# Memory attention of a two-block transformer kernel: where the squares of the state are summed, and the order of the heads' turns and values

## The chip, the cores and the metric

The kernel runs on one core of one Trainium2 chip. The metric is the device time of one execution in microseconds; three runs of the kernel before gave a median of 2088.11 us (2086.93 to 2088.28). The whole computation is one launch with one instruction stream per engine: TensorE (PE), VectorE (DVE), ScalarE (ACT), GpSimd (POOL), and SyncE (SP), which only issues the transfers.

## The reference, cut to what matters

The kernel computes two blocks (a convolution and forgetting attention, a cross attention to a memory, an MLP, and then a second block) on 512 tokens of width 1024. The change lies in the cross attention of the first block:

```python
def memory_cross_attention(h, mem_n, w_mq, w_mk, w_mv, w_mo):      # h = rms_norm(x, norm_mem_pre)
    q = (h @ w_mq).reshape(B, S, MEM_HEADS, MEM_HEAD_DIM)          # 512 tokens, 4 heads of 128
    k = (mem_n @ w_mk).reshape(B, N_MEM, MEM_HEADS, MEM_HEAD_DIM)  # 256 memory rows
    v = (mem_n @ w_mv).reshape(B, N_MEM, MEM_HEADS, MEM_HEAD_DIM)
    logits = jnp.einsum("bqhd,bmhd->bhqm", q, k) * (MEM_HEAD_DIM ** -0.5)
    p = jax.nn.softmax(logits, axis=-1)
    out = jnp.einsum("bhqm,bmhd->bqhd", p, v).reshape(B, S, MEM_INNER)
    return out @ w_mo

def rms_norm(x, g):
    return x * rsqrt(mean(x * x, -1) + 1e-6) * g
```

The root of the mean square of a token is a factor on all its logits. The kernel therefore forms `q` from `x * g` alone, and multiplies the logits by the token's factor inside the exponential.

## The kernel before, in words

State and activations lie feature by feature: eight tiles of 128 features by 512 tokens. Every fp32 product is made of three products of parts (high times low, low times high, high times high, `mm3`), so one 128x128 by 512 step of a product is three matmuls. After each product that feeds another, ACT copies the PSUM bank to a rounded high part and DVE subtracts it to get the low part (`high` and `low`).

Each engine has its own instruction list, written out by hand, and runs it in order. Semaphores that are counted through names (`up`, `at`) connect the lists. PSUM has eight banks, which TensorE takes in turn; `open_bank` waits until the tenant of eight banks ago is free. There is no planner: what stands next in an engine's list runs next, or blocks those behind it.

The stage at issue, on TensorE (lines 981 to 1010):

- `mem_v`: values of the memory. `mem_q(n)`: the queries of head n, eight steps or 24 matmuls; heads 0 and 1 are made together first. `mem_s(h)`: the logits of head h, four blocks of 128 tokens by 256 memory rows, 12 matmuls into two banks. It needs the high part of the queries (ACT, `mq_high`) and the low part (DVE, `mq_out`).
- `column_sum` of the tiles in its list: for each tile four products of 128 tokens with a matrix of ones of 96 columns, so that token sums land one per partition. The four products of a tile are fp32, and each shows as two matmul records. Here it sums the one tile `Y1[0]`, into which DVE has added the squares of all eight tiles of the state (`add_squares`, the last of its seven additions is named `hacc 1 7`).
- `mem_t(h)`: eight transposes that turn the probabilities (tokens by memory rows) of head h. It needs the normalised probabilities, of which ACT makes block 0 (`mem_norm`) and DVE blocks 1 to 3 (`mem_rcp`). `mem_pv(h)`: the values weighted with them, six matmuls, which needs both parts of the turned probabilities (`mem_turned` on ACT, `mem_low` on DVE).
- then `gemm("wm")`, the output product with `w_mo`, 96 matmuls in two chunks of weights of 48.

On ACT (lines 1738 to 1761): `root` takes the square root of the sums, `mem_exp(h)` four exponentials with their sums, and the functions named above. The exponential of head h waits for the head's negated and scaled maximum. On DVE (lines 2515 to 2545): `inverse` (reciprocal of the root), two multiplications that make the scales, `mem_max` (two maxima for a head), `mem_scale` (maxima times scale), and the functions named above. `mem_out(h)` on ACT and DVE makes the two parts of a head's output from the bank of `mem_pv(h)`, and frees it.

POOL makes the low parts of most weights at this place: `w_mq`'s second chunk, then `w_mo`'s first, each in four pieces.

Of the kernel before, what the change touches and what calls it, by code (L numbers as in the profile page):

```python
# [286 lines left out]
def build(nc, t):  # L287
# [9 lines left out]
    with es:  # L297
# [214 lines left out]
        def tensor_program(pe):  # L512
# [35 lines left out]
            def column_sum(parts, nb=4, first=0):  # L548


                for group, ap, need, freed, done in parts:
                    ps = bank(*group) if group in begun else open_bank(*group, hold=True)
                    pe.wait_ge(*at(*need))
                    for b in range(nb):
                        ins = pe.mm(ps[:, SUMW * b:SUMW * b + SUMW], ap[:, blk(first + b)], ONE[:, 0:SUMW],
                                    group not in begun and b == 0,
                                    done is not None, shared=True)
                    begun.add(group)
                    if freed and done:
                        ins.then_inc(*up(acc, ("tf", *freed), done))  # L560
                    elif freed:
                        ins.then_inc(*up(acc, ("tf", *freed)))
                    elif done:
                        ins.then_inc(*up(acc, done))
                    if done:
                        close(*group)
# [377 lines left out]
            def mem_q(n):  # L944
                w = CH["w_mq"][1]
                wh, wl = chunk(w)
                ps = open_bank("mq", n)
                for k in range(8):
                    col = (2 * k + n % 2) * 128
                    pe.wait_ge(*at("hn", 1, k))  # L950
                    ins = pe.mm3(ps[:], wh[:, col:col + 128], wl[:, col:col + 128], *feat(k), k == 0, k == 7)
                ins.then_inc(*up(acc, ("mq", n), *[("w_used", w)] * (n % 2)))

            def mem_s(h):
                for i in range(4):
                    c = 256 * (i % 2)
                    if c == 0:
                        ps = open_bank("ms_", h, i // 2)
                    pe.wait_ge(*at("qm", h))
                    pe.wait_ge(*at("km", h))  # L960
                    ins = pe.mm3(ps[:, c:c + 256], QMH[:, h, blk(i)], QML[:, h, blk(i)], KMH[:, h, :], KML[:, h, :],
                                 True, True)
                    if c:
                        ins.then_inc(*up(acc, ("ms_", h, i // 2)))

            def mem_t(h):
                for j in range(2):
                    ps = open_bank("mt", h, j)
                    for i in range(4):
                        pe.wait_ge(*at("mp", h, i))  # L970
                        ins = pe.turn(ps[:, blk(i)], PM[h % 2][:, i, blk(j)], IDT[:])
                    ins.then_inc(*up(acc, ("mt", h, j)))

            def mem_pv(h):
                ps = open_bank("mo", h)
                for j in range(2):
                    pe.wait_ge(*at("pm", h, j))
                    pe.wait_ge(*at("vm", j))
                    ins = pe.mm3(ps[:], VMH[:, j, blk(h)], VML[:, j, blk(h)], PMH[h % 2][:, j, :], PML[h % 2][:, j, :],
                                 j == 0, j == 1)  # L980
                ins.then_inc(*up(acc, ("mo", h)))
# [10 lines left out]
                close("mq", n)  # L992
            mem_v(1, 1)
            mem_s(0)
            mem_q(2)
            mem_s(1)
            column_sum([(("st", 1), Y1[:, 0, :], ("hacc", 1, 7), None, ("st", 1))])
            mem_q(3)
            mem_s(2)
            mem_t(0)  # L1000
            mem_t(1)
            mem_s(3)
            mem_pv(0)
            mem_t(2)
            mem_pv(1)
            mem_t(3)
            mem_pv(2)
            mem_pv(3)
# [332 lines left out]
        def scalar_program(act):  # L1341
# [364 lines left out]
            def mq_high(n):  # L1706
                act.wait_ge(*at("mq", n))
                high(QMH[:, n, :], bank("mq", n)[:], ("qm", n))

            def mem_exp(h):  # L1710
                slot = 32 * (h % 2) + 160
                for i in range(4):
                    if h >= 2:
                        act.wait_ge(*at("mt", h - 2, 1))
                    act.wait_ge(*at("max", "ms_", h))
                    act.act(PM[h % 2][:, i, :], bank("ms_", h, i // 2)[:, 256 * (i % 2):256 * (i % 2) + 256], ACT.Exp,
                            SM[:, 20 + i:21 + i], SM[:, slot + i:slot + i + 1], SM[:, slot + 4 + i:slot + 5 + i]).then_inc(
                        *out(("exp", "ms_", h, i), *[("free", "ms_", h, i // 2)] * (i % 2)))

            def mem_norm(h):  # L1720

                for i in range(1):
                    s, p = 32 * (h % 2) + 168 + i, PM[h % 2][:, i, :]
                    act.wait_ge(*at("rcp", "ms_", h))
                    act.act(p, p, ACT.Identity, SM[:, s:s + 1]).then_inc(*out(("mp", h, i)))

            def mem_turned(h):
                for j in range(2):
                    act.wait_ge(*at("mt", h, j))
                    if h >= 2:  # L1730
                        act.wait_ge(*at("mo", h - 2))
                    high(PMH[h % 2][:, j, :], bank("mt", h, j)[:], ("pm", h, j))

            def mem_out(h):
                act.wait_ge(*at("mo", h))
                high(OMH[:, h, :], bank("mo", h)[:], ("om", h))
# [3 lines left out]
            mem_v_high(0)  # L1740
            mem_v_high(1)
            weights(CH["w_mo"][0])
            mq_high(2)
            root(("st", 1), 0, "eps6")
            mem_exp(0)
            mem_norm(0)
            mem_exp(1)
            mq_high(3)
            mem_norm(1)
            mem_turned(0)  # L1750
            mem_exp(2)
            mem_turned(1)
            mem_norm(2)
            mem_exp(3)
            mem_out(0)
            mem_turned(2)
            mem_norm(3)
            mem_out(1)
            mem_turned(3)
            mem_out(2)  # L1760
            mem_out(3)
# [321 lines left out]
        def vector_program(dve):  # L2083
# [375 lines left out]
            def add_squares(s, Y, start=1, end=7):  # L2459

                for k in range(start, end + 1):
                    dve.wait_ge(*at("hsq", s, k))
                    if k > 1:
                        dve.wait_ge(*now(dve_tile))
                    dve.tt(Y[:, 0, :], Y[:, 0, :], Y[:, k, :], ALU.add).then_inc(*out(("hacc", s, k)))
# [7 lines left out]
            def mem_v_low(b):  # L2473
                low(VML[:, b, :], bank("mv", b)[:], VMH[:, b, :], ("vm", b), ("free", "mv", b))

            add_squares(1, Y1, 1, 2)


            def mq_out(n):
                low(QML[:, n, :], bank("mq", n)[:], QMH[:, n, :], ("qm", n), ("free", "mq", n))  # L2480

            def mem_max(h):

                s = 32 * (h % 2) + 160
                for b in range(2):
                    dve.wait_ge(*at("ms_", h, b))
                    dve.rmax(SM[:, s + 2 * b:s + 2 * b + 2],
                             bank("ms_", h, b)[:].rearrange("p (a c) -> p a c", a=2)).then_inc(*out(("mmax", h)))

            def mem_scale(h):  # L2490

                s = 32 * (h % 2) + 160
                dve.wait_ge(*at("mmax", h))
                dve.wait_ge(*at("mscale"))
                dve.tt(SM[:, s:s + 4], SM[:, s:s + 4], SM[:, 24:28], ALU.mult).then_inc(*out(("max", "ms_", h)))
# [11 lines left out]
            def mem_low(h):  # L2507
                for j in range(2):
                    low(PML[h % 2][:, j, :], bank("mt", h, j)[:], PMH[h % 2][:, j, :], ("pm", h, j),
                        ("free", "mt", h, j))  # L2510

            def mem_out(h):
                low(OML[:, h, :], bank("mo", h)[:], OMH[:, h, :], ("om", h), ("free", "mo", h))
# [2 lines left out]
            mq_out(1)  # L2516
            mem_v_low(0)
            mem_v_low(1)
            add_squares(1, Y1, 3, 7)
            mem_max(0)  # L2520
            mq_out(2)
            mem_max(1)
            inverse(("st", 1), 0, [("rs1",)])
            dve.wait_ge(*at("rs1"))
            dve.ts(SM[:, 24:28], SM[:, 4:8], -MEM_SCALE, None, ALU.mult).then_inc(*out())
            dve.ts(SM[:, 20:24], SM[:, 4:8], MEM_SCALE, None, ALU.mult).then_inc(*out(("mscale",)))
            mem_scale(0)
            mem_scale(1)
            mem_rcp(0)
            mem_rcp(1)  # L2530
            mq_out(3)
            mem_max(2)
            mem_scale(2)
            mem_low(0)
            mem_max(3)
            mem_scale(3)
            mem_rcp(2)
            mem_low(1)
            mem_rcp(3)
            mem_out(0)  # L2540
            mem_low(2)
            mem_out(1)
            mem_low(3)
            mem_out(2)
            mem_out(3)
# [1067 lines left out]
```

## Time and profile before

| what | value |
|---|---|
| three runs, median (lowest to highest) | 2088.11 us (2086.93 to 2088.28) |
| the profiled execution, its time | 2087.23 us |
| the profiled execution, its span | 2085.4 us |
| TensorE clock granted in it, mean | 0.992 |
| PE busy, share of the span | 2009.2 us, 96% |
| DVE busy | 1271.7 us, 61% |
| ACT busy | 858.6 us, 41% |
| POOL busy | 983.8 us, 47% |

PE, PEld, DVE, ACT, POOL and SP are TensorE's matmuls, its weight loads, VectorE, ScalarE, GpSimd and SyncE. L159 is line 159 of the kernel, often that of a helper: L158 and L159 are where all matmuls are issued, L167 the transposes, L182 all two-tensor operations, L173, L175 and L176 ACT's operations. Tiles are named without their numbers, so `Y` holds the squares, `QMH` and `QML` the two parts of the queries, `KMH` and `KML` those of the keys, `PM` the probabilities, `PMH` and `PML` the two parts of the turned ones, `OMH` and `OML` those of the output, `SM` the small vectors. Matmuls are pipelined: a record is longer than the step from its start to the next start. Times in a timeline are from the start of the span.

### The profile page before, as it was taken

The numbers are of one execution on the slowest core, as the hardware profiler recorded it, in microseconds if no ns is written. First come the engines' busy times: TensorE is split into PE (matmuls) and PEld (weight loads), VectorE is DVE, ScalarE is ACT, GpSimd is POOL, SyncE is SP. The second block draws the span as 40 slices with busy tenths as digits, with TensorE's granted clock in tenths as the row PEclk, the third lists the DMA queues.
The fourth block names the chain that finished last, engine by engine and source line by source line (L and its number), as shares of the span: only waits on it lengthen the run. The fifth ranks groups of instructions, "written<-read, shape, count | busy, mean of one in ns | idle before, by whom it ended". The sixth has DMA issues, their size and how long they took to land.

```text
span 2085.4 us, 23731 instructions
## 1 busy us (share of the span) xinstructions
PE 2009.2 (96%) x9691; PEld 1672.7 (80%) x9691; DVE 1271.7 (61%) x1568; ACT 858.6 (41%) x1250; POOL 983.8 (47%) x486
## 2 busy tenths in 40 slices
PE   7999999899999999999999999999998999999997
PEld 5777888788888877887888888878887888888886
DVE  8678727452344445562777775455579667777643
ACT  5847764621122235773433333242322244333322
POOL 5578554453444333113444444345667644444443
PEclk9999999999999999999999999999999999999999
DMA  6422123112222221021122222224222312223221
GB/s 206 176 104 81 62 82 115 67 61 101 101 88 95 101 98 44 22 71 61 61 101 101 96 88 100 101 81 171 82 71 101 122 66 96 101 101 101 82 101 41
DMA packets 35040, 193.00 MB, mean 93 GB/s; under 512 B 4399, under 2 KB 4991, under 8 KB 15412
## 3 DMA queue, kind: packets, MB, share of 16 engines
q1 hardware_dynamic: 34932, 191.49, 26.2%
q8 instruction: 76, 1.25, 0.3%
q14 instruction: 32, 0.26, 0.0%
HBM read 177.77 MB, written 13.64 MB: 92 GB/s over the span
## 4 chain that ended last, share of the span: by engine, by line
PE 81%; DVE 10%; ACT 4%; POOL 3%; issue 1%; DMA 0%; ACTq 0%; SPq 0%; DVEq 0%; POOLq 0%
PE ps L159 77%; PE ps L158 4%; DVE TMP L182 1%; POOL WL L182 1%; DVE X L182 1%; DVE ps L194 1%; DVE X L194 1%; PE ps L167 1%; DVE YL L182 1%; POOL YF L182 1%; ACT WH L175 0%; DVE VG L182 0%; ACT PM L173 0%; DVE HL L194 0%; POOL CO L182 0%
## 5 line engine op out<-in xcount | busy, mean ns | idle before, releaser
L182 POOL TENSOR_TENSOR WL<-W,WH 128x2048 fp32r<-128x2048 f32 (+3 forms) x172 | 648.3, 3776 | 867.2 <-ACT WH L175 863.7
L159 PE MATMUL ps<-HH,WL 128*128 128x512 f32 (+1 forms) x1392 | 539.1, 387 | 17.1 <-DVE HL L194 7.9
L159 PE MATMUL ps<-HL,WH 128*128 128x512 f32 (+1 forms) x1392 | 532.4, 382 | 0.0
L159 PE MATMUL ps<-HH,WH 128*128 128x512 f32 (+1 forms) x1392 | 532.4, 382 | 0.0
L175 ACT ACTIVATE WH<-W 128x2048 fp32r<-128x2048 f32 (+2 forms) x144 | 267.6, 1858 | 312.9 <-PE ps L159 312.9
L159 PEld LDWEIGHTS ps<-HH,WL 128*128 128x128 f32 x1392 | 262.2, 188 | 76.1 <-DVE HL L194 9.9
L159 PEld LDWEIGHTS ps<-HH,WH 128*128 128x128 f32 x1392 | 262.1, 188 | 51.6
L159 PEld LDWEIGHTS ps<-HL,WH 128*128 128x128 f32 x1392 | 262.3, 188 | 49.5 <-issue 0.2
L182 DVE TENSOR_TENSOR MRL<-MID,MRH 128x512 fp32r<-128x512 f32 x76 | 177.4, 2366 | 162.3 <-ACT MRH L175 162.3
L159 PE MATMUL ps<-MRH,WL 128*128 128x512 f32 x608 | 238.1, 392 | 3.3 <-ACT PAD L175 2.2
L159 PE MATMUL ps<-MRH,WH 128*128 128x512 f32 x608 | 236.7, 389 | 0.0
L159 PE MATMUL ps<-MRL,WH 128*128 128x512 f32 x608 | 236.6, 389 | 0.0
L182 DVE TENSOR_TENSOR MID<-TMP,TMP 128x512 f32<-128x512 f32 x44 | 175.9, 3997 | 30.7 <-ACT TMP L176 30.7
L175 ACT ACTIVATE PAD<-ps 128x512 f32<-128x512 f32 x88 | 52.6, 601 | 273.0 <-PE ps L159 273.0
L194 DVE SCALAR_TENSOR_TENSOR TMP<-PAD,PAR,TMP 128x512 f32<-128x512 f32 x176 | 140.8, 800 | 6.2
L159 PEld LDWEIGHTS ps<-MRH,WL 128*128 128x128 f32 x608 | 114.2, 188 | 28.5 <-ACT PAD L175 3.0
L159 PEld LDWEIGHTS ps<-MRH,WH 128*128 128x128 f32 x608 | 114.1, 188 | 24.0
L159 PEld LDWEIGHTS ps<-MRL,WH 128*128 128x128 f32 x608 | 114.2, 188 | 23.6 <-issue 0.5
L194 DVE SCALAR_TENSOR_TENSOR X<-X,ps 128x512 f32<-128x512 f32 (+1 forms) x36 | 22.5, 628 | 110.3 <-PE ps L159 110.2
L182 POOL TENSOR_TENSOR TMP<-TMP,TMP 128x512 f32<-128x512 f32 x47 | 62.4, 1327 | 57.3 <-ACT TMP L176 55.5
L182 DVE TENSOR_TENSOR TMP<-ps,TMP 128x512 f32<-128x512 f32 x36 | 24.8, 689 | 104.8 <-PE ps L159 98.3
L188 DVE TENSOR_SCALAR TMP<-PAD,PAR 128x512 f32<-128x512 f32 x88 | 42.3, 481 | 72.2 <-ACT PAD L175 72.2
(368 smaller groups left out, 3317.1 us busy)
## 6 DMA issues: line engine op xcount, KB each, us to landing
W<-in_up SPq DMA_DIRECT2D x44, 1024.0 KB, 4.8
W<-in_down SPq DMA_DIRECT2D x22, 1024.0 KB, 4.8
W<-in_w_up SPq DMA_DIRECT2D x16, 1024.0 KB, 4.8
W<-in_w_down SPq DMA_DIRECT2D x16, 1024.0 KB, 4.8
W<-in_hy_in SPq DMA_DIRECT2D x12, 1024.0 KB, 4.9
kd<-STG SPq DMA_DIRECT2D x36, 256.0 KB, 2.0
KB<-kd SPq DMA_DIRECT2D x8, 1024.0 KB, 5.3
W<-in_win_ag SPq DMA_DIRECT2D x4, 1024.0 KB, 5.2
```

Source lines behind the costliest of these rows:

```text
L158: return self.eng.matmul(out, lhs, rhs, start=start, stop=stop, skip_group_check=True)
L159: return self.eng.matmul(out, lhs, rhs, start=start, stop=stop)
L167: return QUIET if self.eng is None else self.eng.transpose(out, src, ident)
L175: return self.eng.activation(out, src, fn, scale=scale)
L182: return QUIET if self.eng is None else self.eng.tensor_tensor(out, a, b, op)
L188: return self.eng.tensor_scalar(out, a, s1, None, o1)
L194: return self.eng.scalar_tensor_tensor(out=out, in0=a, scalar=s, in1=b, op0=o1, op1=o2)
```

## The change

Three things change, in this one stage.

1. DVE adds only the squares of tiles 1 to 3 into `Y1[0]`, all three ahead of `mq_out(0)` (before: two there, and five behind `mem_v_low(1)`). TensorE sums `Y1[0]` and the tiles 4 to 7 by themselves in one group of five column sums, placed right behind `mem_s(0)` (before: one column sum behind `mem_s(1)`).
2. The order of turns and values on TensorE: `mem_t(0)` ahead of `mem_q(3)`, `mem_t(1)` ahead of `mem_s(2)`, `mem_pv(0)` ahead of `mem_s(3)`, `mem_pv(1)` ahead of `mem_t(2)`.
3. The lists of ACT and DVE follow: the root, the exponentials and the normalisation of head 0 stand ahead of the queries of head 2, those of head 1 ahead of the queries of head 3; `mem_out(0)` on DVE stands ahead of `mem_rcp(3)`.

```diff
@@ tensor_program
             mem_v(1, 1)
             mem_s(0)
+            column_sum([(("st", 1), Y1[:, 0, :], ("hacc", 1, 3), None, None),
+                        *[(("st", 1), Y1[:, k, :], ("hsq", 1, k), None, ("st", 1) if k == 7 else None)
+                          for k in range(4, 8)]])
             mem_q(2)
             mem_s(1)
-            column_sum([(("st", 1), Y1[:, 0, :], ("hacc", 1, 7), None, ("st", 1))])
+            mem_t(0)
             mem_q(3)
+            mem_t(1)
             mem_s(2)
-            mem_t(0)
-            mem_t(1)
+            mem_pv(0)
             mem_s(3)
-            mem_pv(0)
+            mem_pv(1)
             mem_t(2)
-            mem_pv(1)
             mem_t(3)
             mem_pv(2)
             mem_pv(3)
@@ scalar_program
             weights(CH["w_mo"][0])
-            mq_high(2)
             root(("st", 1), 0, "eps6")
             mem_exp(0)
             mem_norm(0)
+            mq_high(2)
             mem_exp(1)
-            mq_high(3)
             mem_norm(1)
             mem_turned(0)
+            mq_high(3)
+            mem_turned(1)
             mem_exp(2)
-            mem_turned(1)
             mem_norm(2)
             mem_exp(3)
             mem_out(0)
-            mem_turned(2)
             mem_norm(3)
             mem_out(1)
+            mem_turned(2)
             mem_turned(3)
@@ vector_program
-            add_squares(1, Y1, 1, 2)
+            add_squares(1, Y1, 1, 3)
@@
             mem_v_low(1)
-            add_squares(1, Y1, 3, 7)
             mem_max(0)
-            mq_out(2)
-            mem_max(1)
             inverse(("st", 1), 0, [("rs1",)])
             dve.wait_ge(*at("rs1"))
             dve.ts(SM[:, 24:28], SM[:, 4:8], -MEM_SCALE, None, ALU.mult).then_inc(*out())
             dve.ts(SM[:, 20:24], SM[:, 4:8], MEM_SCALE, None, ALU.mult).then_inc(*out(("mscale",)))
             mem_scale(0)
+            mem_rcp(0)
+            mq_out(2)
+            mem_max(1)
             mem_scale(1)
-            mem_rcp(0)
             mem_rcp(1)
+            mem_low(0)
             mq_out(3)
+            mem_low(1)
             mem_max(2)
             mem_scale(2)
-            mem_low(0)
             mem_max(3)
             mem_scale(3)
             mem_rcp(2)
-            mem_low(1)
+            mem_out(0)
             mem_rcp(3)
-            mem_out(0)
+            mem_out(1)
             mem_low(2)
-            mem_out(1)
             mem_low(3)
```

## Rows read from the trace of the kernel before

**Rows 1.** The page: busy time, and the chain that ended last, by engine.
```profile
PE 2009.2 (96%) x9691; PEld 1672.7 (80%) x9691; DVE 1271.7 (61%) x1568; ACT 858.6 (41%) x1250; POOL 983.8 (47%) x486
PE 81%; DVE 10%; ACT 4%; POOL 3%; issue 1%; DMA 0%; ACTq 0%; SPq 0%; DVEq 0%; POOLq 0%
```
**Rows 2.** Busy time by stretch: the stage from mem_s(0) to the output product.
```profile
351.68:383.83 32.15, 27.77 (x162) 23.42 (x160) 25.33 (x52) 21.76 (x54) 6.65 (x5) 1.00 0.20 66
```
**Rows 3.** What PE waited for, 350 to 388: total, times, longest.
```profile
PE ps L167 <- ACT PM L176: 3.2, 3, 1.5
PE ps L159 <- ACT PM L173: 0.9, 1, 0.9
```
**Rows 4.** Timeline of PE: start us, us, operation [idle before <-releaser].
```profile
351.68 0.28 PE L159 MATMUL ps<-KMH,QML 128*128 128x256 f32 x1
...
353.11 0.40 PE L159 MATMUL ps<-HH,WL 128*128 128x512 f32 x1
...
358.58 0.28 PE L159 MATMUL ps<-KMH,QML 128*128 128x256 f32 x1
...
360.49 1.10 PE L158 MATMUL ps<-ONE,Y 128*128 128x96 f32 x8 [0.32 <-DVE Y L182]
361.38 0.48 PE L159 MATMUL ps<-HH,WL 128*128 128x512 f32 x1
361.70 0.39 PE L159 MATMUL ps<-HL,WH 128*128 128x512 f32 x1
...
366.94 0.28 PE L159 MATMUL ps<-KMH,QML 128*128 128x256 f32 x1
...
368.37 1.03 PE L167 MATMUL ps<-IDT,PM 128*128 128x128 f32 x8
...
380.07 1.09 PE L167 MATMUL ps<-IDT,PM 128*128 128x128 f32 x8 [1.49 <-ACT PM L176]
380.93 0.48 PE L159 MATMUL ps<-PMH,VML 128*128 128x512 f32 x1
...
383.83 0.39 PE L159 MATMUL ps<-OMH,WL 128*128 128x512 f32 x1
```
**Rows 5.** Timeline of PE, a column sum of three tiles.
```profile
405.59 2.81 PE L158 MATMUL ps<-ONE,TMP 128*128 128x96 f32 x24
```
**Rows 6.** Timeline of DVE.
```profile
347.09 3.47 DVE L182 TENSOR_TENSOR Y<-Y 128x512 f32<-128x512 f32 x2
350.48 1.27 DVE L182 TENSOR_TENSOR QML<-ps,QMH 128x512 fp32r<-128x512 f32 x2
...
370.81 1.28 DVE L207 TENSOR_REDUCE SM<-ps 128x2 f32<-128x512 f32 x2
```
**Rows 7.** Shortest, median and longest of the squares' additions, 346 to 362.
```profile
L182 DVE TENSOR_TENSOR Y<-Y x5: 692/1659/1772, 347.1 to 355.3; 128x512 f32<-128x512 f32 x5
```
**Rows 8.** Timeline of POOL.
```profile
344.87 6.84 POOL L182 TENSOR_TENSOR WL<-W,WH 128x512 fp32r<-128x512 f32 x4
...
388.03 4.60 POOL L182 TENSOR_TENSOR WL<-W,WH 128x2048 fp32r<-128x2048 f32 x1 [26.56 <-ACT WH L175]
```
**Rows 9.** Timeline of ACT.
```profile
361.63 0.26 ACT L176 ACTIVATE SM<-ps,PAR 128x4 f32<-128x4 f32 x1 [2.25 <-PE ps L158]
361.92 1.28 ACT L173 ACT_TABLE_LOAD   x1
363.93 0.56 ACT L173 ACTIVATE PM<-ps,SM 128x256 f32<-128x256 f32 x1 [0.73 <-DVE SM L182]
364.49 0.56 ACT L173 ACTIVATE PM<-ps,SM 128x256 f32<-128x256 f32 x1
...
372.31 0.57 ACT L173 ACTIVATE PM<-ps,SM 128x256 f32<-128x256 f32 x1 [1.29 <-DVE SM L182]
...
379.45 0.57 ACT L176 ACTIVATE PM<-PM,SM 128x256 f32<-128x256 f32 x1
379.85 0.66 ACT L175 ACTIVATE OMH<-ps 128x512 fp32r<-128x512 f32 x1
```

## The prediction, made before the result was known

> **What bounds the kernel now.** The page comes first: PE is busy for 96% of the span and holds 81% of the chain that ended last [rows 1]. So PE time that is added anywhere is paid for unless PE was waiting there, and a wait is worth at most what PE stands idle. Second, the stretch of the change, from `mem_s(0)` at 351.68 to the first matmul of the output product at 383.83: 32.15 us, PE busy for 27.77, so 4.38 idle, at the full granted clock (1.00, which is 2.4 GHz) [rows 2]. Third, what PE waited for: 3.2 us in three waits before transposes, for the normalised probabilities, and 0.9 before `mem_pv(0)` [rows 3]; before the column sum that the change makes earlier it is only 0.32 [rows 4]. Fourth, the timelines of the engines, to see which wait ends last. Behind the stage PE starts 96 matmuls of the output product, and all that follows depends on them; so the change is worth what it does to the start at 383.83.
>
> **The prices.** From starts [rows 4]: `mem_s` 353.11 - 351.68 = 1.43 us; `mem_q(2)` 358.58 - 353.11 = 5.47; `mem_q(3)`, behind another kind of matmul, 366.94 - 361.38 = 5.56, as its first step takes 0.32 instead of 0.23; eight transposes 380.93 - 380.07 = 0.86. A column sum of one tile takes 361.38 - 360.49 = 0.89. The one of three tiles lasts 2.81 to the end of its last record [rows 5]; from 361.38 against 360.49 + 1.10 a last record reaches 0.21 us past the next start, so that is 2.60, or 0.87 a tile. I take 0.885 for a tile, 4.42 us for five.
>
> **Part 1, the squares.** The change adds four tiles, 32 matmul records, 3.53 us of PE. It takes four additions from DVE, which are on no list that PE waits for except the column sum's own. In return the sum stands earlier. But a third addition now stands ahead of `mq_out(0)`, and behind that low part are `mq_out(1)`, `mem_v_low` and all of DVE's list; on PE `mem_s(0)` waits for it, and everything behind. In the trace two additions last from 347.09 to 350.56, `mq_out(0)` starts at 350.48 and `mem_s(0)` 1.20 later, with no idle time before it [rows 4, 6]. The third addition costs between 0.69 (the shortest of these rows) and 1.77 (the longest) [rows 7]. The long ones run while POOL makes low parts of weights, from 344.87 to 351.71 [rows 8]; the third would start at 350.58, inside that. I take the long one: the addition ends at 352.35, `mq_out(0)` at 352.98 (0.68 after a start at 352.30), `mem_s(0)` starts at 353.02, 1.34 late, and I let its first step cost 0.1 more, as the first behind another kind did at 361.38. By the short end PE would wait 0.3 us instead.
>
> The Trainium skill (SBUF — State Buffer, Who interferes with whom) says that the port pair that VectorE and GpSimd share is an exclusive lock: a VectorE instruction with two SBUF inputs waits for the whole of a GpSimd instruction that reads SBUF. The trace agrees, since additions come at 0.69 or at about 1.66 us and none between [rows 7], and by it the third addition waits until POOL is done at 351.71 and ends at 352.4, as taken. If the two shared bandwidth instead, it would end at about 352.0 and the sum below would be 0.35 less.
>
> **Part 2, PE's list up to the logits of head 2.** From 351.68: wait and restart 1.44, `mem_s(0)` 1.43, five column sums 4.42 (done 358.97), `mem_q(2)` 5.56 (done 364.53), `mem_s(1)` 1.43 (365.96), `mem_t(0)` 0.87 (366.83), `mem_q(3)` 5.56 (372.39), `mem_t(1)` 0.86 (373.25), `mem_s(2)` 1.51, as it follows transposes and its first step costs 0.08 more (374.76). Nothing in this list waits a second time: the probabilities of head 0 are there early, as follows, and those of head 1 at about 371. In the kernel before `mem_s(2)` ended at 368.37 [rows 4]. So it is 6.4 us late.
>
> **Part 3, the scale, sooner.** The root starts at 359.15 instead of 361.63. In the kernel before the table load of 1.28 lay beside DVE's work and the first exponential waited another 0.73 for DVE [rows 9]; now DVE waits with `mem_scale(0)` right behind the inverse, and the table load is what is late: `mem_exp(0)` starts at 360.75, 3.2 us sooner than 363.93. That gain ends there. `mem_exp(1)` needs the logits of head 1, which PE finishes at 365.96 behind the column sums and `mem_q(2)`, and DVE must first make `mq_out(2)`, which waits until ACT's `mq_high(2)` can start at 364.7. DVE: 365.3 to 365.9, two maxima to 367.1, scale; `mem_exp(1)` starts at about 367.3, where it started at 366.89. Head 1 is then normalised at about 370.5, so `mem_t(1)` finds it ready.
>
> **Part 4, from the logits of head 2 to the end.** `mq_high(3)` starts at 372.57, `mq_out(3)` 373.19 to 373.79, two `mem_low(1)` to 374.99, then `mem_max(2)`. From there to the exponential it was 372.31 - 370.81 = 1.50 [rows 6, 9]; so `mem_exp(2)` starts at 376.49, 4.18 us later than before. The rest was 383.83 - 372.31 = 11.52 us [rows 4, 9]. Now, counted from `mem_exp(2)`: four exponentials at about 0.55, then reciprocal and normalisation of 0.40 [rows 9], `mem_exp(3)` at +2.93 (its maxima are ready at +1.9), `mem_out(0)` on ACT at +5.12 and on DVE to +6.35, only then `mem_rcp(3)`, the normalisation at +6.56, `mem_out(1)` at +6.97, `mem_turned(2)` at +7.46; DVE's `mem_out(1)` to +8.19 and its first `mem_low(2)` to +8.87; `mem_pv(2)` and `mem_pv(3)` take 383.83 - 380.93 = 2.90 [rows 4], so the output product starts at +11.81, 0.29 more. Before, `mem_exp(3)` stood 3.54 behind `mem_exp(2)`, but its reciprocal did not wait for `mem_out(0)`: the gain of one is lost by the other. The wait for the transposes of head 3 grows from 1.49 to about 3.0 us.
>
> **The sum.** 4.18 + 0.29 = 4.5 us, the product's start at 388.3. Check by PE alone: 3.53 added, and waits of 4.38 become about 5.4 (1.4 before `mem_s(0)`, about 1 before `mem_t(2)`, 3 before `mem_t(3)` and `mem_pv(2)`). The second chunk of `w_mo` is no new wait: POOL has its low part at 388.03 + 4.60 = 392.63 [rows 8], PE wants it 48 steps of 0.227 after 383.83, at 394.7, and both move together, since ACT's copy stands behind the last `mem_out`. No transfer is moved. Nothing downstream has slack that PE's start could eat, PE being busy for 96%. Against the profiled execution, 2087.23 + 4.5 = 2091.7; the median of the runs shown is 0.9 above that execution, so 2088.11 + 4.5 = **2092.6 us**. Ends: the short third addition takes off 1.0 (3.4); a bank or a queue that I ordered wrongly by one operation of 0.6 on the path from head 2 adds 0.6 to 1.2 (5.7).
>
> **Rivals.**
> (a) *The waits absorb it.* PE stood idle for 4.38 us and 3.53 is added; if the earlier scale moves the whole chain of probabilities by its 3 us, all exponentials start early, PE's waits before the transposes go, and the added work lies in their place: from nothing to +0.9, 2088.1 to 2089.0. For it: the three waits before transposes are the largest [rows 3]. Against: only head 0 is early; heads 1 and 2 wait for PE itself.
> (b) *The other side, not slower.* The same mechanism to its end: PE never waits from 351.68 on and needs only 27.77 + 3.53 = 31.30 us, 0.85 less than now: 2087.3. It decides from the point where `mem_exp(2)` starts by 371. Against: the third addition alone gives PE a new wait, and `mem_s(2)` is behind 23 us of PE's work. Even so it is within 0.2%.
> (c) *Cheap column sums.* A record of 96 columns steps at 0.11 us [rows 4, 5]. If in a long group its 96 columns alone set the pace, 0.04 us each at 2.4 GHz, the 40 records would take 1.6 instead of 4.4, and the sum falls to +1.7: 2089.8. Against: the 24 of one group kept 0.11, and so do records of other widths, the transposes of 128 columns with 0.86/8 = 0.107 and the logits of 256 with 1.43/12 = 0.119 [rows 4]; something that all have in common, not the columns, sets it. The Trainium skill (TensorE: Matmul & The Clock Gate, Back-to-back issue gap) has about 81 ns for a pair of weight load and matmul at 128 columns; by that the 40 records take 3.2 us, an estimate, and the forecast falls to +3.3, 2091.4. No row of this trace shows that pace.
> (d) *More than forecast.* DVE's queue from `mem_low(1)` to `mem_max(2)`, and `mem_out(0)` ahead of `mem_rcp(3)`, each wait for ACT, which waits for PE: if one of these hand-overs is missed, +5.7 to +7, 2093.8 to 2095.
>
> **How the numbers follow.** About 0.2% (4.2 us) is what a measurement of this kernel can tell from no change. The forecast (+3.4 to +5.7) has 0.74, of which I put 0.48 above 4.2 us and 0.26 below, since 4.5 is close to that bound. (a) has 0.10, (b) 0.03, (c) 0.03, (d) 0.08, and 0.02 is left for faster by a cause that I don't see. Slower: 0.48 + 0.08 = 0.56; same: 0.26 + 0.10 + 0.03 + 0.03 = 0.42; faster 0.02. The range adds half a microsecond of the runs' spread to both ends and leaves out (a), (b) and half of (d): 2090.6 to 2094.3.
>
> **What would show it.** An idle time of 1.0 to 1.4 us before `mem_s(0)`, with a low part of the queries as its releaser; a group of 40 records of 128x96 from about 354.5, 4.4 us long; the table load between root and first exponential with no wait behind it; `mem_s(2)` ending 6 us later than 368.37, `mem_exp(2)` at about 376.5; one long wait of about 3 us before the transposes of head 3; the first matmul with `OMH` at 388.3. A start of the product below 386 would make the prediction wrong, and if `mem_exp(2)` is then early, its third and fourth part.

## The result and the profile after

The changed kernel takes 2093.76 us (median of nine runs, 2091.8 to 2095.16) against 2088.11 (nine runs, 2086.36 to 2089.06): 1.0028 times the time, 95% interval 1.002 to 1.0036, so 5.65 us more. The forecast was 2092.6, in the range 2090.6 to 2094.3. The profiled execution took 2091.94 us with a span of 2090.1, the second fastest of the nine. The median lies 1.8 above it, and that turns out to matter.

The page of after, span and busy time, in the columns of [rows 1]:
```profile
span 2090.1 us, 23786 instructions
PE 2010.9 (96%) x9723; PEld 1673.4 (80%) x9723; DVE 1267.7 (61%) x1564; ACT 859.1 (41%) x1250; POOL 982.3 (47%) x486
```
Exactly 32 matmul records more on PE and four instructions fewer on DVE. Spans are not the place to read the difference, though: the stage begins at 353.39 here and at 351.68 before, with no line changed ahead of it that TensorE waits for (e10, whose only edit lies in the stage, begins it at 353.15), and it ends 2090.1 - 390.36 = 1699.7 us before the span does, against 2085.4 - 383.83 = 1701.6. These two differences, +1.7 and -1.9 us, nearly cancel in this pair. So each kernel below is read by the length of its stage, from the end of the last `mem_v` product (its last start plus 0.227) to the first matmul of the output product.

The stage of after, to hold against [rows 2] (columns: PE, PEld, DVE, ACT, POOL busy, granted clock, DMA share, GB/s):
```profile
353.39:390.36 36.97, 32.46 (x194) 28.26 (x194) 21.40 (x49) 22.31 (x54) 4.97 (x5) 0.95 0.17 58
385.00:388.40 3.40, 3.24 (x12) 2.76 (x13) 3.25 (x7) 2.65 (x6) 0.00 (x0) 0.55 0.00 0
```
It lasts 36.97 us instead of 32.15: 4.82 more. And the clock column is new: 0.95 over the stage and 0.55 in its last part, where it was 1.00.

PE's timeline of after, answering to [rows 4]:
```profile
354.62 0.39 PE L159 MATMUL ps<-KMH,QML 128*128 128x256 f32 x1 [1.06 <-DVE QML L182]
...
356.16 2.82 PE L158 MATMUL ps<-ONE,Y 128*128 128x96 f32 x24
358.81 1.95 PE L158 MATMUL ps<-ONE,Y__178 128*128 128x96 f32 x16
360.54 0.47 PE L159 MATMUL ps<-HH,WL 128*128 128x512 f32 x1
...
376.20 0.40 PE L159 MATMUL ps<-PMH,VML 128*128 128x512 f32 x1
...
381.14 1.14 PE L167 MATMUL ps<-IDT,PM 128*128 128x128 f32 x8 [0.57 <-ACT PM L176]
385.16 1.97 PE L167 MATMUL ps<-IDT,PM 128*128 128x128 f32 x8 [2.88 <-ACT PM L176]
386.97 0.79 PE L159 MATMUL ps<-PMH,VML 128*128 128x512 f32 x1
387.56 0.63 PE L159 MATMUL ps<-PML,VMH 128*128 128x512 f32 x1
...
390.36 0.39 PE L159 MATMUL ps<-OMH,WL 128*128 128x512 f32 x1
```
`mem_s(0)` starts 354.62 - 353.39 = 1.23 us late, behind the low part of the queries. The 40 records of column sums take 360.54 - 356.16 = 4.38. `mem_s(2)` ends at 376.20, which is 22.81 of the stage against 16.69 before, 6.12 later. PE does not wait from `mem_s(0)` until the transposes of head 2 (0.57), and waits 2.88 before those of head 3. Those eight transposes take 386.97 - 385.16 = 1.81 instead of 0.86, and the values of heads 2 and 3 390.36 - 386.97 = 3.39 instead of 2.90. The slow transposes cost the stage nothing here: in e6 below they take 0.86, and PE then waits 0.67 for VectorE's low part, so the values of head 2 start no sooner.

ACT's timeline of after, answering to [rows 9]:
```profile
361.08 1.28 ACT L173 ACT_TABLE_LOAD   x1
362.37 0.56 ACT L173 ACTIVATE PM<-ps,SM 128x256 f32<-128x256 f32 x1
...
369.06 0.56 ACT L173 ACTIVATE PM<-ps,SM 128x256 f32<-128x256 f32 x1 [2.15 <-DVE SM L182]
...
378.04 0.56 ACT L173 ACTIVATE PM<-ps,SM 128x256 f32<-128x256 f32 x1 [2.37 <-DVE SM L182]
```
Counted from the start of the stage, the first exponential of head 0 stands at 8.98 (12.25 before, 3.3 sooner), that of head 1 at 15.67 (15.21 before), that of head 2 at 24.65 (20.63 before, 4.02 later). The gain of the earlier scale ends at the first head. The additions of squares, answering to [rows 7]: all three that are left are slow ones, the third too.
```profile
L182 DVE TENSOR_TENSOR Y<-Y x3: 1665/1665/1773, 348.8 to 352.3; 128x512 f32<-128x512 f32 x3
```

### The profile page after: what moved, and what is told of

It reads as the page before. It is cut to its first block, busy times and chain, and to the rows that moved or that the text cites. A ratio compares the mean times of both kernels' runs of the same rounds, so it can differ in the third digit from the quotient of the medians.

```text
span 2090.1 us, 23786 instructions
## 1 busy us (share of the span) xinstructions
PE 2010.9 (96%) x9723; PEld 1673.4 (80%) x9723; DVE 1267.7 (61%) x1564; ACT 859.1 (41%) x1250; POOL 982.3 (47%) x486
## 4 chain that ended last, share of the span: by engine, by line
PE 80%; DVE 10%; POOL 4%; ACT 4%; issue 1%; DMA 0%; ACTq 0%; SPq 0%; DVEq 0%; POOLq 0%
PE ps L159 76%; PE ps L158 4%; DVE TMP L182 1%; POOL WL L182 1%; DVE X L182 1%; DVE ps L194 1%; PE ps L167 1%; POOL X L182 1%; DVE X L194 1%; DVE YL L182 1%; POOL YF L182 1%; DVE HL L194 1%; ACT WH L175 0%; DVE VG L182 0%; POOL CO L182 0%
## 5 line engine op out<-in xcount | busy, mean ns | idle before, releaser
L159 PEld LDWEIGHTS ps<-MRH,WL 128*128 128x128 f32 x608 | 114.1, 188 | 28.4 <-ACT PAD L175 3.0
```

The lines of the kernel that those rows point to most:

```text
L159: return self.eng.matmul(out, lhs, rhs, start=start, stop=stop)
```

## The experiments

Two notions of the loss are tested: PE's own order with its added work (the theory), and either part by itself being the whole of it. From e5 on, the half clock is a question of its own.

**e1, the sums alone.** The five early sums with the turns and values in the order of before (TensorE's part of the edit is shown; the lists of ACT and DVE follow it).
```diff
 mem_s(0); column_sum(five tiles)
-mem_q(2); mem_s(1); mem_t(0); mem_q(3); mem_t(1); mem_s(2); mem_pv(0); mem_s(3); mem_pv(1); mem_t(2); mem_t(3)
+mem_q(2); mem_s(1); mem_q(3); mem_s(2); mem_t(0); mem_t(1); mem_s(3); mem_pv(0); mem_t(2); mem_pv(1); mem_t(3)
```


> The five early column sums alone (three additions on VectorE, tiles 4 to 7 on TensorE, root and inverse ahead of the queries of head 2), turns and values of the heads in the order of before. The stage from mem_s(0) to the output product was 32.15 us before and 36.97 after. Theory (the change costs by TensorE's own order: 3.53 us of added matmuls, 1.3 us of waiting for the third addition, and turns that now stand ahead of the logits of heads 2 and 3): one turn less stands ahead of mem_s(2), so mem_exp(2) starts about 2 us sooner than after; stage 34.3 us, +2.1 over before, time about 2090.5. Rival (the early sums are all of the loss, the order is free): stage about 37, +4.8, time 2093. Rival (the early sum helps by itself and the new order spoils it): stage under 32.

Measured: stage 34.73 us (+2.58), time 2091.33 us, 1.0013 of before (1.0003 to 1.0022). `mem_exp(2)` at 23.21 of the stage, 1.44 sooner than after. The clock is 1.00 throughout the stage (the stage's busy times, then what PE waited for):
```profile
353.30:388.03 34.73, 31.19 (x193) 27.07 (x193) 20.89 (x49) 21.89 (x54) 4.96 (x5) 1.00 0.18 62
```
```profile
PE ps L167 <- ACT PM L176: 2.4, 2, 1.5
```
```profile
374.35 1.91 PE L167 MATMUL ps<-IDT,PM 128*128 128x128 f32 x16
```
Both turns, not one, have left the place ahead of `mem_s(2)`: its end, where these transposes start, is at 374.35 - 353.30 = 21.05 of the stage, 1.76 sooner than after. From `mem_exp(2)` to the output product it is 34.73 - 23.21 = 11.52 us, as before. One limit of the edit: on ACT the exponentials of head 0 still stand behind `mq_high(2)`, so `mem_exp(0)` starts at 368.12, 14.82 of the stage (12.25 before). The early sum brings no early exponential here, and the rival that it would help by itself isn't tested in full. An estimate bounds it: `mem_exp(2)` stood 24.65 - 22.81 = 1.84 behind its logits in after; with that it would come at 22.9 here, 0.3 sooner.

**e2, the order alone.** VectorE adds all squares and TensorE sums one tile behind `mem_s(1)`, as before; the rest as after.
```diff
 mem_s(0)
-column_sum(five tiles)
 mem_q(2)
 mem_s(1)
+column_sum(Y1[0], with all squares added)
 mem_t(0)
```


> The new order of turns, values, exponentials alone; VectorE adds all squares as before and TensorE sums one tile behind mem_s(1) as before. Theory: no matmul is added, but mem_t(0) now stands ahead of mem_q(3) and has to wait for the exponentials of head 0, which start about 363 only: one new wait of about 4.8 us before the transposes of head 0, the waits of 0.6 and 3 us before those of heads 2 and 3 as after; stage 36.8 us, +4.6, time about 2092.7, so each part alone costs about as much as both. Rival (the loss is the added matmuls and the third addition, nothing else): stage 32 to 33, time 2088 to 2089.

Measured: stage 41.66 us (+9.5), time 2098.03 us (four runs), 1.0048 (1.0032 to 1.0065). The wait before the transposes of head 0 is there at the size expected, but behind it and behind the one of head 3 the matmuls run slowly (busy times of the stage and of 7 us in it, then PE's timeline):
```profile
351.90:393.56 41.66, 33.17 (x161) 27.96 (x160) 26.24 (x52) 22.19 (x54) 6.63 (x5) 0.84 0.14 51
366.40:373.40 7.00, 6.87 (x22) 5.83 (x23) 4.27 (x12) 4.33 (x13) 0.00 (x0) 0.57 0.00 1
```
```profile
366.53 1.97 PE L167 MATMUL ps<-IDT,PM 128*128 128x128 f32 x8 [4.72 <-ACT PM L176]
368.15 0.78 PE L159 MATMUL ps<-HH,WL 128*128 128x512 f32 x1
368.72 0.63 PE L159 MATMUL ps<-HL,WH 128*128 128x512 f32 x1
369.15 0.63 PE L159 MATMUL ps<-HH,WH 128*128 128x512 f32 x1
```
A step is 0.43 us instead of 0.227 (368.72 to 369.15), half the clock, that is the 1.2 GHz level, and the granted clock over 7 us is 0.57. The eight transposes and `mem_q(3)` take 1.62 + 7.57 instead of 0.86 + 5.56 us, the last values 4.77 instead of 2.90: 4.6 us together. Without them the stage would be 37.0, the expected size. So the theory on the order held, and a term was missing from it.

**e3, the price of four tiles.** After, with tiles 4 to 7 left out of the sum.
```diff
-column_sum([(("st", 1), Y1[:, 0, :], ("hacc", 1, 3), None, None), *[... for k in range(4, 8)]])
+column_sum([(("st", 1), Y1[:, 0, :], ("hacc", 1, 3), None, ("st", 1))])
```


> The kernel after, with the squares of tiles 4 to 7 left out of the sum (the scale is computed from tiles 0 to 3 alone), so 32 matmul records fewer and all else the same. Theory: TensorE's list decides when mem_exp(2) starts, so all 3.53 us come back; stage 33.4 us, mem_exp(2) 3.5 us sooner, +1.2 over before, time about 2089.5. Rival (the softmax chain decides and the added matmuls lie in waits): stage 36 to 37, time 2093.

Measured: `mem_exp(2)` at 21.04, 3.61 us sooner than after (3.53 expected); stage 34.84, more than the 33.4 expected, because the last values took 4.87 us at half clock. At 2.90 it would be 32.87. Time 2089.9, 1.001 (1.0 to 1.0019). All of the added matmuls' time comes back: none of it lay in a wait.

**e4, the normalisation of head 3 ahead of the outputs.**
```diff
 ACT: mem_exp(3)
-mem_out(0); mem_norm(3); mem_out(1); mem_turned(2); mem_turned(3)
+mem_norm(3); mem_turned(2); mem_out(0); mem_out(1); mem_turned(3)
 DVE: mem_rcp(2)
-mem_out(0); mem_rcp(3); mem_out(1); mem_low(2); mem_low(3)
+mem_rcp(3); mem_low(2); mem_out(0); mem_out(1); mem_low(3)
```


> The kernel after with the normalisation of head 3 ahead of the outputs of heads 0 and 1 on ScalarE and VectorE (mem_norm(3) and mem_turned(2) ahead of mem_out(0); mem_rcp(3) and mem_low(2) ahead of it). Theory: the wait before the transposes of head 3 falls from 2.9 to about 2.0 us, the output product starts 0.5 us sooner by that. The half clock that the trace of after shows from 385 on, behind that wait, cost another 0.5; if it followed the wait it may go, if it is a matter of chance it may lie elsewhere. Stage 36.0 to 36.5 us, time 2092.5 to 2093.5. Rival (the order on VectorE between rcp(3) and out(0) is what costs): stage 34 or less.

Measured: the wait before the transposes of head 3 is 1.80 instead of 2.88, and a new one of 0.59 comes before `mem_pv(2)`, whose bank `mem_out(0)` frees. Stage 38.06 us, longer than after, time 2093.88, as after. The last values took 4.99 us at half clock; with 2.90 the stage would be 35.97, 0.5 under after without its own loss (36.97 - 0.49 = 36.48), as expected. A wait shortened by 1.1 us did not keep the clock up: it is 1.00 from 380.6 to 382.4 and 0.50 from 382.7, ahead of the wait of 0.59. PE's timeline:
```profile
382.43 1.81 PE L167 MATMUL ps<-IDT,PM 128*128 128x128 f32 x8 [1.80 <-ACT PM L176]
384.84 0.80 PE L159 MATMUL ps<-PMH,VML 128*128 128x512 f32 x1 [0.59 <-DVE OML L182]
```

**e5, after once more**, unchanged, to see whether the short slow stretch of its first profile is the usual case.

> The kernel after, unchanged, beside the others of this call. Its first profile had half a clock for 3.4 us in the stage, which began in the wait before the transposes of head 3 and cost 0.5 us of the 36.97. The three kernels with the same last waits (e2, e3, e4) had 6.8 us of it there and paid 1.3 to 1.9. Theory (the waits bring the clock down, and the first profile caught the shorter case): half clock again from that wait on, stage 37.0 to 38.4 us, median time 2093 to 2094.5. Rival (chance, no tie to the wait): no half clock in the stage, stage 36.5, and the median is where it was for another reason.

Measured: stage 38.24 us, time 2094.4 (seven runs, 2092.04 to 2095.24), 1.0028. The same waits to 0.01 us, and half clock from 385 for twice as long as in the first profile (busy times of three stretches, then PE's timeline):
```profile
353.65:391.89 38.24, 33.74 (x193) 29.20 (x193) 21.55 (x49) 22.31 (x54) 4.96 (x5) 0.91 0.16 56
385.00:392.00 7.00, 6.60 (x21) 5.37 (x22) 4.49 (x9) 3.48 (x7) 0.00 (x0) 0.56 0.00 0
414.00:430.00 16.00, 12.52 (x62) 9.99 (x61) 11.81 (x17) 7.28 (x13) 12.16 (x10) 0.89 0.33 117
```
```profile
385.40 1.97 PE L167 MATMUL ps<-IDT,PM 128*128 128x128 f32 x8 [2.88 <-ACT PM L176]
387.21 0.79 PE L159 MATMUL ps<-PMH,VML 128*128 128x512 f32 x1
...
391.89 0.39 PE L159 MATMUL ps<-OMH,WL 128*128 128x512 f32 x1
```
The last values take 4.68 us; at 2.90 the stage would be 36.46, the first profile's 36.48 again. So the structure costs 4.3 us, and the clock 0.5 in the one execution and 1.8 in the other. The longer slow stretch looks like the usual case: of the six profiles whose transposes of head 3 wait 1.80 us or more, unfilled, five (e2, e3, e4, e5, e7) have last values of 4.68 to 4.99 us and only the first profile of after has 3.39. The mean granted clock of an execution can't tell the two apart, since half clock elsewhere moves it as well: e4's profile has the longer stretch and a mean of 0.993, the first profile of after 0.994, e5's 0.990.

**e6, the wait filled.** After, with twelve products that add no result between the transposes of heads 2 and 3.
```diff
 ps = open_bank("mt", h, j)
+if (h, j) == (3, 0):
+    keep_busy(12, CH["w_mo"][0], "mt", 3, 0)
```


> The kernel after with twelve products (ONE identity times weights, 0.227 us each, into the bank that the transposes of head 3 then overwrite) put between the transposes of heads 2 and 3, where TensorE waits 2.9 us. They add no result and lie in the wait. Theory (the half clock follows the wait): no half clock in the stage, the transposes of head 3 take 0.86 again, values of heads 2 and 3 2.9 us; stage 36.5 us, time about 2092 or a little less, 1 to 2 us under the kernel after of the same call. Rival (the half clock comes at that place whatever TensorE does): as after, 37 to 38.4 us, 2093.9.

Measured: stage 36.41 us, granted clock 1.00, time 2091.81, 1.002 (1.001 to 1.003), 2.6 under e5 on the same chip. Busy times, then PE's timeline:
```profile
353.15:389.56 36.41, 33.99 (x205) 29.28 (x205) 21.36 (x49) 22.20 (x54) 4.95 (x5) 1.00 0.16 59
414.00:430.00 16.00, 12.35 (x52) 8.41 (x51) 13.90 (x19) 8.21 (x14) 12.16 (x9) 1.00 0.22 66
```
```profile
381.78 3.01 PE L158 MATMUL ps<-WH,IDR 128*128 128x512 f32 x12
384.91 1.14 PE L167 MATMUL ps<-IDT,PM 128*128 128x128 f32 x8
386.72 0.50 PE L159 MATMUL ps<-PMH,VML 128*128 128x512 f32 x1 [0.67 <-DVE PML L182]
```
The exponentials and the values came no sooner; only PE was kept at work. That rules out the rival: the half clock in the stage follows the wait. The stage gives 38.24 - 36.41 = 1.83 us. The medians differ by 2.6, the means of the runs (2094.06 and 2092.25) by 1.8, so the gain has the size of what the stage shows.

The stretch from 414 explains nothing. Its clock is 0.89 in e5 and 1.00 in e6, but it is 1.00 in the first profile of after too, where no wait is filled:
```profile
414.00:430.00 16.00, 12.40 (x57) 8.69 (x55) 13.35 (x18) 7.41 (x13) 12.16 (x10) 1.00 0.22 77
```
And it costs nothing there. The same VectorE operation stands 449.91 - 391.89 = 58.02 us behind the first output product in e5, and 447.63 - 389.56 = 58.07 in e6 (the first line is e5's, the second e6's):
```profile
449.91 0.69 DVE L182 TENSOR_TENSOR TMP<-ps,TMP 128x512 f32<-128x512 f32 x1 [6.58 <-ACT TMP L175]
447.63 0.69 DVE L182 TENSOR_TENSOR TMP<-ps,TMP 128x512 f32<-128x512 f32 x1 [6.58 <-ACT TMP L175]
```
These two profiles (2095.24 us, the slowest of e5's runs, and 2091.05, the fastest of e6's) do differ behind the stage, by 1.9 us, but late: the granted clock from 1580 to 1600 is 0.91 in e5 and 1.00 in e6. It is 1.00 in the first profile of after as well, so the filling is not shown to be the cause.

The Trainium skill (TensorE: Matmul & The Clock Gate, What's actually happening) says that the gate passes pulses by how busy the engine has been recently. These pairs of profiles agree: the same products, 1.00 with the wait filled, and 0.56 in the seven microseconds from 385 in e5, where it is not.

**e7, no third addition.** After, with six tiles summed by TensorE, 0 and 3 to 7.
```diff
-add_squares(1, Y1, 1, 3)
+add_squares(1, Y1, 1, 2)
-("hacc", 1, 3) ... for k in range(4, 8)
+("hacc", 1, 2) ... for k in range(3, 8)
```


> The kernel after with six tiles summed by TensorE (0 with the squares of 1 and 2 added, and 3 to 7), so that no third addition stands ahead of the queries' low parts. Theory: mem_s(0) starts without a wait (1.23 us back, and 0.1 of its first step), eight more records cost 0.88, mem_exp(2) starts 0.4 to 0.5 us sooner; stage 36.5 us where the clock is as in the first profile of after (36.97), up to 37.9 where it is as in e4; time 0.5 us under after. Rival (the third addition is a main cause): stage under 36 by itself.

Measured: `mem_s(0)` starts without a wait, `mem_exp(2)` at 24.21, 0.44 sooner. Stage 38.02, of which 1.98 at half clock, so 36.04 without; time 2094.17, as e5. The third addition cost 1.23 us of waiting and 0.1 of the first step, the eight records that spare it cost 0.9; the difference of 0.4 is what comes back.

**e8, the queries first.** Nothing is added to PE; VectorE adds all seven squares at once.
```diff
 TensorE
-mem_s(0); mem_q(2); mem_s(1); column_sum(Y1[0]); mem_q(3); mem_s(2); mem_t(0); mem_t(1); mem_s(3); mem_pv(0); mem_t(2); mem_pv(1); mem_t(3)
+mem_q(2); column_sum(Y1[0]); mem_s(0); mem_s(1); mem_q(3); mem_s(2); mem_t(0); mem_t(1); mem_s(3); mem_pv(0); mem_pv(1); mem_t(2); mem_t(3)
 ScalarE (from mq_high(2) on)
+root; mq_high(2); mem_exp(0); mem_exp(1); mem_norm(0); mem_norm(1); mq_high(3); mem_turned(0); mem_exp(2); mem_turned(1)
+mem_exp(3); mem_norm(2); mem_norm(3); mem_turned(2); mem_out(0); mem_turned(3); mem_out(1)
 VectorE
+add_squares(1, Y1, 1, 7); mq_out(0); mq_out(1); mem_v_low(0); mem_v_low(1); inverse and scales; mem_max(0); mem_scale(0)
+mem_max(1); mem_scale(1); mq_out(2); mem_rcp(0); mem_rcp(1); mem_max(2); mq_out(3); mem_scale(2); mem_low(0)
+mem_max(3); mem_scale(3); mem_rcp(2); mem_low(1); mem_rcp(3); mem_low(2); mem_low(3); mem_out(0) to mem_out(3)
```


> A new order that adds nothing to TensorE. VectorE adds all seven squares at once; meanwhile TensorE makes the queries of head 2 (they need nothing of VectorE), then the one column sum, then the logits of heads 0 and 1; both exponentials stand together; each normalisation and turn stands ahead of the outputs. Theory (the column sum belongs early but behind work that waits for nobody, and no product may stand ahead of the logits that VectorE's maxima wait for): no wait before mem_s(0), the root at +6.5 us of the stage instead of +9.95 before and +7.4 after, mem_exp(2) at +17.7 instead of +20.6, the remaining waits of TensorE about 1.6 instead of 4.4 us; stage 28.4 us, 3.8 less than before, and with no long wait no half clock in it: time about 2084. Rival (the exponentials and maxima set the pace and the order of TensorE is free): stage 31.5 to 32.2, time 2087.5 to 2088.

Measured: stage 29.35 us, 2.80 less than before (3.8 expected), PE busy for 27.70 of it; time 2084.99 us, 0.9986 of before (0.9976 to 0.9995). It beats both kernels. Its median is 3.7 us under that of before's runs beside it (2088.68); the ratio says 2.9 us, 1.0 to 5.0. Busy times, then PE's longest wait:
```profile
351.70:381.05 29.35, 27.70 (x161) 23.35 (x161) 24.42 (x53) 21.80 (x55) 5.32 (x5) 1.00 0.20 72
414.00:430.00 16.00, 15.54 (x62) 11.25 (x63) 14.94 (x18) 9.07 (x13) 10.30 (x7) 1.00 0.00 0
```
```profile
PE ps L159 <- ACT PM L173: 1.3, 1, 1.3
```
`mem_exp(2)` starts at 18.0 of the stage (before 20.63). The largest wait left is one of 1.3. The missing 1.0 us of the expectation is an error of its sum: it expected waits of 1.6 instead of 4.4 us, and 29.35 - 27.70 = 1.65 is what PE stands idle. With the 27.77 us that PE was busy before, waits of 1.6 make a stage of 29.4, not 28.4. The profiled execution is one of e8's slower ones (2086.01 us) and spends 2084.2 - 381.05 = 1703.2 us behind the stage, 1.6 more than before's; the gain of the stage is thus not read from the two spans.

**e9, one part of e8.** Before, with all seven additions at once and `mem_q(2)` ahead of `mem_s(0)`.
```diff
+mem_q(2)
 mem_s(0)
-mem_q(2)
-mem_s(1)
 column_sum(Y1[0])
+mem_s(1)
-add_squares(1, Y1, 1, 2) ... add_squares(1, Y1, 3, 7)
+add_squares(1, Y1, 1, 7)
```


> The kernel before with two things alone of e8: VectorE adds all seven squares at once ahead of the queries' low parts, and TensorE makes the queries of head 2 ahead of mem_s(0), with the one column sum behind mem_s(0). All other orders as before. Theory (most of e8's gain is the work that waits for nobody standing first, so that the sum is ready when TensorE comes to it and costs no more products): root at +7.9 of the stage, mem_exp(2) at +19.0, stage 30.5 us, 1.6 less than before; time 2086.5 to 2087, less if the half clock behind the stage goes too. Rival (the gain of e8 is in the turns and outputs of the last heads): stage 32, time as before.

Measured: stage 30.91 us, 1.24 less than before, `mem_exp(2)` at 19.37. Time 2087.16 against 2088.69, ratio 0.9998 (0.9989 to 1.0006): by the runs no difference can be told. By the stage it is 44% of e8's gain; the rest is in the other orders.

**e10, the wait of before filled** with six products.

> The kernel before with six products (1.4 us) in its 1.49 us wait before the transposes of head 3, which add no result. The profile of before has no half clock in the stage but 3.4 us of it from 417, behind the waits of the next norm; the filled kernel of after and e8 have none there. Theory (a fall of the clock follows waits that lie shortly before it, so a fuller stage can spare the next one): stage 32.15 to 32.3 us as before, no half clock at 417, time 0.5 to 1.5 us under before. Rival (the half clock at 417 comes from the waits of 406 to 410 alone): as before, 2088.

Measured: stage 32.16 us, time 2088.33, ratio 0.9999 (0.999 to 1.0008), and the half clock behind the stage stays. The rival's time came true: before has no loss by the clock in this stage that filling could give back. Its mechanism is not shown: the kernel after, unchanged, has half clock behind the stage in one profile (e5) and none in the other. The stretch behind the stage:
```profile
414.00:430.00 16.00, 13.20 (x50) 10.28 (x50) 15.38 (x20) 8.71 (x14) 9.75 (x6) 0.89 0.15 60
```

| kernel | stage, us | against before | of it by half clock | time, median us | ratio (95%) |
|---|---|---|---|---|---|
| before | 32.15 | | 0 | 2088.11 | |
| after, first profile | 36.97 | +4.82 | 0.49 | 2093.76 | 1.0028 (1.002 to 1.0036) |
| e5 after again | 38.24 | +6.09 | 1.78 | 2094.4 | 1.0028 (1.0017 to 1.0039) |
| e1 sums alone | 34.73 | +2.58 | 0 | 2091.33 | 1.0013 (1.0003 to 1.0022) |
| e2 order alone | 41.66 | +9.51 | 4.6 | 2098.03 | 1.0048 (1.0032 to 1.0065) |
| e3 tiles left out | 34.84 | +2.69 | 1.97 | 2089.9 | 1.001 (1.0 to 1.0019) |
| e4 rcp first | 38.06 | +5.91 | 2.09 | 2093.88 | 1.0027 (1.0018 to 1.0036) |
| e6 wait filled | 36.41 | +4.26 | 0 | 2091.81 | 1.002 (1.001 to 1.003) |
| e7 no third addition | 38.02 | +5.87 | 1.98 | 2094.17 | 1.0029 (1.0018 to 1.004) |
| e8 queries first | 29.35 | -2.80 | 0 | 2084.99 | 0.9986 (0.9976 to 0.9995) |
| e9 part of e8 | 30.91 | -1.24 | 0 | 2087.16 | 0.9998 (0.9989 to 1.0006) |
| e10 before, filled | 32.16 | +0.01 | 0 | 2088.33 | 0.9999 (0.999 to 1.0008) |

The ratios hold each kernel against runs of before made beside it, with medians of 2088.11 (after), 2088.04 (e1 to e4), 2088.68 (e5 to e8) and 2088.69 (e9, e10), and are not the quotients of the medians. Stages are from one profile each. The half clock's share is the excess of the last values over 2.90 us, in e2 also that of the slow stretch behind head 0's transposes.

## Why the prediction was right, and the term that it lacked

- *Part 1.* The third addition is a slow one and `mem_s(0)` starts 1.23 us late (forecast 1.34). The five sums take 4.38 (4.42). e3 gives their price on the path: 3.61 for 32 records (3.53).
- *Part 2.* Right, `mem_s(2)` ends 6.12 later (forecast 6.4). PE runs without a wait from `mem_s(0)` to the values of head 1, and its list decides when the logits of head 2 are there; e1 takes two turns from ahead of them; they are there 1.76 sooner, and `mem_exp(2)` comes 1.44 sooner.
- *Part 3.* Right: the table load ends at 362.36 and the first exponential starts at 362.37, 3.3 us sooner (3.2), and head 1 gains nothing (15.67 of the stage, forecast 15.6).
- *Part 4.* `mem_exp(2)` came 4.02 later (4.18). From it to `mem_pv(2)` 386.97 - 378.04 = 8.93 us (8.91). The wait before the transposes of head 3 is 2.88 (about 3.0), that of head 2 0.57 (about 1). Moving `mem_rcp(3)` forward was worth 0.5 us, as e4 shows, not more, since `mem_pv(2)` then waits for its bank.
- *The sum.* At full clock the stage is 36.41 to 36.48 us, +4.3 against a forecast of +4.5. The term that was too small is "`mem_pv(2)` and `mem_pv(3)` take 2.90": that price came from a stage whose longest wait was 1.49 us. Behind the wait of 2.88, which the text itself forecast, they took 3.39 and 4.68 in the two profiles. That is 0.5 to 1.8 us more, and with it +4.8 to +6.1; the median of the runs says +5.65, 1.2 more than forecast, in line with this. How often the long stretch comes in runs that have no profile is not shown.
- *Luck.* The profiled execution, 2091.94 us, lies 0.2 from what the forecast gives for one like before's (2087.23 + 4.5 = 2091.7). That is closer than the working deserves: it holds the 0.5 us of half clock that the forecast lacked, and +1.7 and -1.9 us outside the stage, which the change doesn't explain.
- *Rivals.* (a) and (b) fell: nothing of the added work lay in waits (e3). (c) fell by the 4.38. (d) came close in size (+5.7 to +7) but not in mechanism: no hand-over between ACT and DVE was missed.
- The two parts are not a sum. At full clock e1 costs 2.6, e2 about 4.9, both 4.3: with the new order the root must be early, or `mem_t(0)` waits 4.72 us ahead of `mem_q(3)`. The early sum buys that wait off with 3.6 us of matmuls and 1.2 of waiting.

## What to carry to other kernels

Where one engine is busy for 96%, bringing a small result forward by giving that engine more work pays only if everything behind it in the chain comes forward too; follow the second and third link, not the first. Look instead for work in that engine's list that waits for nobody, and put it ahead of the products that wait (e8: 2.8 us from order alone). And price the work behind a lengthened wait of TensorE at both levels of its clock.

## What the runs showed that I had not expected

- The granted clock was 0.55 to 0.57 from the end of waits of 2.88 and 4.72 us on, and 0.50 behind one of 1.80 (e4), but 1.00 in stages with a last wait of 1.49 or 1.50 (before, e1). A step of 512 columns was 0.43 us there instead of 0.227. The slow stretch cost 0.5 us of the stage in one execution of the same kernel and 1.8 in another.
- Twelve useless products in a wait saved 2.6 us of the median and 1.8 of the mean (e6 against e5). In before, with nothing to lose in the stage, six of them saved nothing (e10).
- Half clock also stands behind the stage, from about 417 in before and e10 (0.89 over 414 to 430), and likewise in e5, but not in the first profile of after, in e6 and in e8. It differs between two executions of one kernel, so the stage alone does not decide it; what does stays open. In e5 it cost nothing.
